# The down weights of each layer's expert 30 sent as one transfer of 64 rows and eight of 8 rows

## The reference

```python
for i in range(2):
    h = rms_norm(x, norm_mix_g[i])
    x = x + (pool_mixer(h, ...) if i == 0 else diff_attention(h, ...))
    h = rms_norm(x, norm_ffn_g[i])
    x = x + hier_moe(h, ...)      # 32 experts, each token goes to 2
return rms_norm(x, final_g)

def expert_block(args):           # of hier_moe
    xb, e = args
    a = jax.nn.silu(xb @ w1[e]) * (xb @ w3[e])   # w1, w3: 1024 x 512
    return a @ w2[e]                             # w2: 512 x 1024
```

## Time and profile before

| What | Value |
|---|---|
| Median of 3 runs | 1104.18 us (1101.11 to 1104.31) |
| Span of the profiled execution, first to last instruction | 1099.3 us |
| DMA, mean over the span | 388 GB/s |
| PE busy | 871.6 us, 79% |
| DVE busy | 351.2 us, 32% |
| ACT busy | 225.6 us, 21% |

### The profile page before, as it was taken

How to read it: one execution, slowest core, us unless ns; L and a number is a source line. 1 busy time by engine, 2 the same in 40 slices (tenths; PEclk the granted TensorE clock), 3 DMA queues, 4 the chain that set the end, 5 groups by cost and what they waited for, 6 DMA issues and landing times.

```text
span 1099.3 us, 18770 instructions
## 1 busy us (share of the span) xinstructions
PE 871.6 (79%) x8132; PEld 512.5 (47%) x8132; DVE 351.2 (32%) x863; ACT 225.6 (21%) x547; POOL 1.2 (0%) x8
## 2 busy tenths in 40 slices
PE   6878776777685868789999988988877766776885
PEld 5744433344343434444787554444534433443442
DVE  3623322323132322222257363322332313232323
ACT  3411211111111111112134332211212111111102
POOL 0000000000000000000000000000000000000000
PEclk9789988989798989999999999999999889897998
DMA  8999999999999999999703678999999999999994
GB/s 343 427 425 424 425 426 427 426 426 427 427 427 427 426 427 427 428 422 421 320 7 120 264 286 361 427 426 426 426 424 425 425 427 427 428 426 427 427 423 191
DMA packets 35587, 426.55 MB, mean 388 GB/s; under 512 B 5394, under 2 KB 6802, under 8 KB 8980
## 3 DMA queue, kind: packets, MB, share of 16 engines
q1 hardware_dynamic: 35476, 424.91, 91.8%
HBM read 423.85 MB, written 1.05 MB: 387 GB/s over the span
## 4 chain that ended last, share of the span: by engine, by line
PE 45%; DMA 38%; DVE 11%; issue 4%; ACT 2%; DVEq 0%; SPq 0%; ACTq 0%
DMA ring<-in_moe_w 37%; PE ps L540 14%; PE ps L588 8%; PE ps L812 5%; PE ps L663 4%; DVE work L1270 3%; PE ps L794 3%; PE ps L473 2%; PE ps L433 2%; PE ps L866 2%; DVE hT L1317 1%; DVE work L1278 1%; PE ps L493 1%; ACT work L986 1%; DVE work L1272 1%
## 5 line engine op out<-in xcount | busy, mean ns | idle before, releaser
L540 PE MATMUL ps<-ring,work 128*32 128x256 f32 x4224 | 284.0, 427 | 137.5 <-DMA ring<-in_moe_w 105.5
L540 PEld LDWEIGHTS ps<-ring,work 128*32 128x32 f32 x4224 | 163.5, 122 | 265.4 <-issue 211.1
L1268 DVE TENSOR_SCALAR work<-work 128x128 f32<-128x128 f32 (+1 forms) x64 | 14.6, 229 | 474.2 <-ACT work L986 474.2
L588 PE MATMUL ps<-ring,work 128*32 128x256 f32 x2032 | 125.2, 388 | 31.6 <-DVE work L1278 30.9
L473 PE MATMUL ps<-work,h_sb 128*128 128x256 f32 x512 | 131.3, 400 | 2.9 <-issue 2.2
L986 ACT ACTIVATE work<-ps 128x256 f32<-128x256 f32 x64 | 24.5, 383 | 504.7 <-PE ps L540 504.7
L1317 DVE COPY hT<-ps 32x512 f32<-32x512 f32 x112 | 76.5, 683 | 133.9 <-PE ps L588 133.1
L473 PEld LDWEIGHTS ps<-work,h_sb 128*128 128x128 f32 x512 | 94.4, 194 | 41.5 <-issue 29.1
L588 PEld LDWEIGHTS ps<-ring,work 128*32 128x32 f32 x2032 | 60.7, 111 | 92.9 <-DVE work L1278 55.5
L998 ACT COPY hT<-ps 32x512 f32<-32x512 f32 x112 | 64.7, 578 | 111.2 <-PE ps L588 110.6
L959 ACT ACTIVATE work<-ps,gcol 128x256 f32<-128x256 f32 (+1 forms) x144 | 58.6, 458 | 110.3 <-PE ps L473 103.9
(11 more groups left out here) (163 smaller groups left out, 467.4 us busy)
## 6 DMA issues: line engine op xcount, KB each, us to landing
ring<-in_moe_w SPq DMA_DIRECT2D x182, 2048.0 KB, 30.5
ring<-in_moe_w SPq DMA_DIRECT2D x15, 1024.0 KB, 30.2
ring<-in_attn_wv SPq DMA_DIRECT2D x2, 2048.0 KB, 33.6
ring<-in_attn_wq SPq DMA_DIRECT2D x2, 2048.0 KB, 32.8
ring<-in_attn_wk SPq DMA_DIRECT2D x2, 2048.0 KB, 33.7
ring<-in_attn_wo SPq DMA_DIRECT2D x2, 2048.0 KB, 36.9
spare<-in_moe_w SPq DMA_DIRECT2D x1, 2048.0 KB, 18.7
x_sb<-in_x SPq DMA_DIRECT2D x2, 512.0 KB, 4.0
```

Of the source, the lines that this page charges most:

```text
L540: mm = pe.matmul(gu_ps[SB * j:SB * (j + 1), b, :, :], xg[:, u, kt, b, k, :], w[:, :, kt, P * j:P * (j + 1)], start=(kt == 0 and b == 0), s ...
L588: mm = pe.matmul(y_ps[SB * i:SB * (i + 1), b, :], actT[:, b, SB * j:SB * (j + 1)], wj[:, 256 * i:256 * (i + 1)], start=(j == 0 and b == 0) ...
```

## The change

```diff
+        s_split = sem("s_split")
...
         LAST_C = CPE * (NE - 1)
 
+        SPLIT_C, SPLIT_ROWS, LOW = LAST_C - 1, 64, 8
+        SPLIT_SIGNALS = (P - SPLIT_ROWS) // LOW * 16
...
                         load_half(layer, c + 2, 0, s_fill)
                         load_half(layer, c + 2, 1, loaded[(c + 2) % RING])
+                    elif c == SPLIT_C:
+
+                        sp.wait_ge(used[(c - RING) % CPE], layer * NE + (c - RING) // CPE + 1)
+                        part, dst = chunk_parts(layer, c // CPE, c % CPE), ring[:, c % RING, :]
+                        sp.dma_start(dst[0:SPLIT_ROWS, :], part[0:SPLIT_ROWS, :]).then_inc(loaded[c % RING], 16)
+                        for r in range(SPLIT_ROWS, P, LOW):
+                            sp.dma_start(dst[r:r + LOW, :], part[r:r + LOW, :]).then_inc(s_split, 16)
                     elif c < LAST_C and (layer == 0 or c not in (EARLY_C, FILL_C)):
                         stream(ITERS - 1, c)
...
                         pe.wait_ge(loaded[c % RING], (u0 + c // RING + 1 - ahead) * 16)
                         if layer == 1 and c == LATE_C + 1:
                             pe.wait_ge(s_early, 16)
+                        if c == SPLIT_C:
+                            pe.wait_ge(s_split, SPLIT_SIGNALS * (layer + 1))
                         return c % RING
```

## The result

The changed kernel takes 1137.16 us (median of 4 runs, 1128.29 to 1137.87), the kernel before 1103.95 us beside it (4 runs, 1101.11 to 1104.31): a ratio of 1.0289, 95% interval 1.0257 to 1.0321. It is 33.2 us slower; "no change" was wrong, and the time lies above the range. The profiled execution took 1137.87 us with a span of 1136.1, that is 36.8 us more than the span of before. It is the longest of its four runs and the profiled one of before (1101.11 us) the shortest, so some 3.6 of these 36.8 us are scatter between runs.

What follows compares the result with a forecast made beforehand. The prediction took DMA engines to pace the expert phases, with chunk 91's landing the last one waited for. All terms were 0, so 1104.2 + 0 gave 1104.2 us, range 1099.5 to 1108.5.

Steps and rivals of the forecast that it cites:

- (a): Chunk 92's rows: eight engines carry 12 rows, others 4, at 0.61 us a row; landings shift 2.45 us, gain 0 us.
- the bold one: End of each layer's experts: chunk 91's landing is the last anything waits for, ahead of everything the change touches.
- Both bounds: Sharing of chunk 92's 8-row pieces: equally over 16 engines, nothing moves; or always the same eight engines, plus and minus 2.45 us.
- the second bound: Each 8-row piece gives one row to each of the same eight engines: 12 rows there, 4 on the others.
- the room of 1.7 us: Chunk 92's landing was 1.7 us ahead of expert 30's down matmuls, in both layers.
- rival A: Late engines are among the eight loaded ones: chunk 92 onward lands 2.45 us later, 3.7 us together, 1107.9 us; chance 0.32.
- nothing to gain: PE waits for none of the landings from chunk 92 on before the change, so landing sooner gains 0 us.
- rival B: Last landings do gate in timed executions; the change returns at most 2.45 us a layer, 4.9 us, 1099.3 us; chance 0.17.
- (b): Eight more transfers on the DMA queue: queued behind others they show no cost of their own, 0 us.
- (c): Eight more SP issues, 3.5 us, 8 at worst, covered by the 30 us queue: 0; attention's lambda loads had 2.2 us room.
- (d): One more semaphore in PE's wait at expert 30's first down matmul: both are up before it, 0 us.
- C: 8-row transfers run on one engine: 36 us a layer, 1176 us; chance 0.02.

Runs made afterwards that it cites:

- two64: Changed kernel with chunk 92 as two transfers of 64 rows, partitions 0 to 63 and 64 to 127, no small pieces: 1128.13 us, ratio to before 1.0245.
- two_even: Changed kernel with chunk 92 as two 64-row transfers, one to the even partitions, one to the odd: 1102.78 us, ratio to before 0.9993.
- low16: Changed kernel with four pieces of 16 rows instead of eight of 8: 1133.44 us, ratio to before 1.0274.
- cols8: Changed kernel with chunk 92 cut by columns, nine transfers of the same sizes, each over all 128 partitions: 1103.67 us, ratio to before 1.0001.
- pieces_low: Changed kernel with even partitions first, then four 8-row pieces to odd partitions below 64, other 32 odd rows left out: 1102.56 us, ratio to before 0.9992.
- pieces_high: Changed kernel with even partitions first, then four 8-row pieces to odd partitions above 64, other 32 odd rows left out: 1111.73 us, ratio to before 1.0075.

## Why the prediction was wrong

**The sentence that failed** is in step (a), that each row costs 0.61 us wherever it is written, and with it the bold one, that chunk 91's landing is ahead of everything the change touches. Both bounds of (a) priced who carries the rows, and none priced where they land. A 16 KB row takes 1.1 to 1.25 us in the median while the 64-row transfer or the pieces are under way, and the engines that are still in chunk 91 slow down with the rest: it lands at 480.80 and not at 473.11. The range came from shifts of 2.45 us and could not hold 12 and 15 us of waiting in the two layers.

**The rule that speaks against the change** was passed over. By SBUF — State Buffer, Door 1: The DMA port swizzle, in the Trainium skill, a write to partitions 0 to 63 goes at about 218 GB/s at best, and by its table of ports one to the even partitions of all 128 uses all ports; the trace agrees, with 222 GB/s in two64 and 422 in two_even. By that rate alone, 1 MB for each half takes 4.8 us instead of 2.45, some 4.7 us a layer for the chunk, as an estimate from that page; less the room of 1.7 us it is 6 us for both layers. It measures 24.5 us in two64, since the other transfers in flight are slowed too and the engines reach the chunk up to 9 us apart: in two64 the packets are slow from 464.4 to about 488 us.

**(a), the sharing.** The landings bear out the second bound, eight engines for an 8-row piece. The eight are some of the early engines and some of the late ones: in layer 0 pieces land from 470.56 us on, when only six engines are through the 64-row transfer, and up to 491.84, 6.5 us behind its last landing (485.38). So rival A's condition, a late engine among the eight, seems to hold, and the sum's, that the eight are the early ones, doesn't. Its price of 2.45 us is too small by the same factor: four rows more at 1.2 us each are 4.9 us a layer. That fits the 9 us between two64 and the change, but low16, which shares its pieces evenly, lies between them at 1133.44 us and the intervals of all three overlap. How much of the last 9 us is the uneven share stays open.

**(a), nothing to gain.** Nothing speaks against it. two_even, cols8 and pieces_low split the chunk without crossing and are within 0.1% of before. The first two leave every engine its share, so they say nothing of rival B, which lives on a smaller share for the late engines. pieces_low takes four rows a layer off eight engines and gains nothing clear of noise (0.9992, 0.9976 to 1.0008); which engines are late in it was not looked into, so B is unlikely and not refuted.

**(b), eight more transfers cost nothing.** It held for the time: cols8, with nine transfers, is at 1.0001. Its DMA share of 0.83 shows that they are not quite free on the queue; the last engine is 0.7 us later, and the room hid that.

**(c), SP.** The issues of after around chunk 92, layer 0:

```profile
447.57 0.56 SPq L382 DMA_DIRECT2D ring<-in_moe_w  x1
448.17 2.84 SPq L384 DMA_DIRECT2D ring<-in_moe_w  x8
...
453.20 4.36 SPq L310 DMA_DIRECT2D ring<-in_moe_w  x1
```

The eight cost 2.84 us where 3.5 was taken. The full queue did hold SP, 4.36 us at one issue in layer 0, and no loss shows for it: the DMA share stays at 1.00 from 455 to 462 us. The lambda loads didn't come to be a wait: DVE waits 1.3 us for the last of attention's small loads where it had waited 7.8 before.

**(d), the semaphore.** As such it costs 0, but it is the wait in which all of the loss stands, since its transfers land 12.1 us behind the 479.73 at which PE had needed them.

**Rival A** named the right place, PE at line 600 in expert 30, with a mechanism that is too small, 1.8 us a layer, and doesn't explain two64, where no engine has more rows than before. **C**, one engine for 8 rows, is refuted by the eight landings of each piece. No term at all stood for slower matmuls behind a wait, which came to 9.4 of the 36.8 us in the profiled execution.

## What to carry to other kernels

When a transfer is cut by partitions, ask of each piece not only how many rows each engine gets but whether it writes in the half of the partitions where it writes in the full transfers: cut into even and odd partitions the rate stays at 420 GB/s, and cut by columns the program's time stays, with gaps in the transfers. Read the GB/s row beside the DMA's busy share, since engines at half speed show as fully busy. And a wait ahead of PE is to be priced with its clock: behind layer 1's 15.2 us the clock was 0.50 for 11 us and 5.2 us came on top. It isn't the same each time, as layer 0's 4.2 us on 12.2 show, half of which may be scatter.

## What was not expected of the hardware

- One part of the traffic slows all of it. Transfers that nobody changed, on engines that had not yet come to the new ones, went from 0.61 to 1.1 us and more a row within a microsecond. A limit on the half that is written (about 220 GB/s for 64 partitions) doesn't explain that alone: with six engines in the new transfer, those that still write the other half should have kept their 0.61 us. In pieces_high one engine in the other half slows only itself and one other (14 of 16 keep 0.61 to 0.67 us), and several slow all. How it spreads from two to sixteen is open. So is whether the crossing itself does it, or two engines that meet on the same way into SBUF; the pair of slow engines speaks for a meeting, and no run here separates the two.
- Queued transfers cost very little each: nine in place of one moved the last landing of the chunk by 0.7 us (cols8, 478.7 against 478.0).
- The engines of one queue were up to 9 us apart: chunk 91 lands on its first engine at 464.4 and on its last at 473.1 in the kernel before. With that spread one slow chunk of 2 MB keeps the traffic slow for some 25 us (464.4 to 491 in after).
